# Square-sum matmuls of the norms moved later in TensorE's order, and a small projection moved ahead of a down-projection

## The chip, the cores and the metric

The kernel runs on one core of one Trainium2 chip. The metric is the device time of one execution in microseconds, lower is better. A core has TensorE (matmuls into eight PSUM banks), VectorE, ScalarE, GpSimd and the SP queue; each runs its own list of instructions in order and meets the others only at semaphores.

## The reference

Two transformer blocks of different kinds, one after the other, on 256 tokens of width 2048, all in fp32. What matters here is where the RMS norms and the residual sums stand:

```python
# first block
a = rmsnorm(h, attn_norm)                       # N_ATTN
h = h + concat(hgrn2, fox, moba of a @ w_in) @ w_out
c = rmsnorm(h, ffn_norm)                        # N_FFN
h = h + (gelu(conv(c @ w_gate)) * (c @ w_up)) @ w_down
e = rmsnorm(h, ple_norm)                        # N_PLE
h = h + sigmoid(e @ w_ple_gate) * (p @ w_ple_proj)
# second block
h2 = rmsnorm(x, attn_norm_g) * (1 + sc1) + sh1  # N_ATTN2
x = x + g1 * (concat(swa, mla of h2) @ w_out)
h2 = rmsnorm(x, mlp_norm_g) * (1 + sc2) + sh2   # N_MLP2
x = x + g2 * (relu(h2 @ w_ff1) ** 2 @ w_ff2)
return rmsnorm(x, final_norm_g)                 # N_FINAL
```

Here `rmsnorm(x, g)` is `x / sqrt(mean(x * x) + eps) * g`, the mean over the 2048 features of a token.

## The kernel before

**Layout.** The residual `x` lies in SBUF as 16 blocks of 128 features by 256 tokens. All weights form one stream of 384 *units* of 1 MB, each of two *halves* of eight 128x128 tiles. SP loads the units into four slots (`raw`) in the order in which the host packs them (`put`, at the end of the file). Each half then goes through ScalarE, which rounds it (`rnd`, line 796, `wh`), and VectorE, which makes the rest (`sub`, line 1251, `wl = raw - wh`); activations are split in the same way (a high and a low part, `xs`, `xc`, `hs`, `px`). TensorE multiplies each tile twice: `wh` by the pair (512 columns) and `wl` by the high part (256 columns), lines 489 to 493. Four slots of `wh` and `wl`; ScalarE and VectorE work three halves ahead of TensorE (`LOOK`), as far as slots come free.

**Units.** `unit(kind, ...)` is TensorE's code of one unit: "full" is one output block of 16 tiles over both halves; "eight" one block of 8 tiles per half; "quad" two blocks of 4 tiles per half (the last down-projection, K of 4 x 128). Output blocks rotate through four PSUM banks; a block waits (`s_evac`) until the one four before it has been taken. For down- and output-projections VectorE adds the block to `x` (`add_blocks`, lines 1301 and 1303); for gates ScalarE copies the low half out (`half_copy`, line 820) and VectorE adds and scales (`take_scaled`, lines 1284 and 1286).

**A norm.** The sum of squares of all 2048 features is made in four groups g of four blocks. ScalarE squares a group (`squares`, line 842), VectorE adds it down to one 128x256 tile (`square_adds`, lines 1376 and 1380) into `sqs`, which has two slots, and TensorE adds over the partitions by a matmul with ones (`square_sums`, line 502) into PS[4], for all four groups. Then ScalarE takes the root (`root`, line 858), VectorE the reciprocal (`rms_ready`, line 1292). Groups 0 to 2 are made early, while blocks of the producing projection are still coming: ScalarE at half `SQ_EIGHT` (5), 9, 13 of the last sixteen halves, VectorE one half later, TensorE one more (halves 7, 11, 15). In the last down it is SQ_QUAD = 3, in the ple gate SQ_PLE = 10 with steps of 8. N_ATTN is made from the input, beside the first two units of work.

**Normed input.** For N_ATTN, N_FFN and N_PLE the norm's factor is applied after the matmul, so that the next projection can begin with `x * gain` (`hi_x` of ScalarE, line 863; `lo_x` of VectorE, line 1360) before the root is there.

**Order around the last down.** Last up units of the ffn, last down (4 "quad" units = 8 halves), side projection `p @ w_ple_proj` (two units, four halves, TensorE lines 695 to 703; the results are copied to `mix` by ScalarE's `proj_take`, line 1139), ple gate (16 full units, `ple_in`, ScalarE's `sigmoid`, `ple_add`), then N_ATTN2. `hi_p` names in the new text the copy of `pin` to `px`, and `lo_p` its low part (line 1702). VectorE also makes products for the second block's modulation (`mods`, line 1319), one or two between halves, all through the first block.

All orders are written out by hand: each engine's list is a Python program that calls its steps at numbered halves.

Of the kernel before, what the change touches and what calls it, by code (L numbers as in the profile page):

```python
# [29 lines left out]
ALU = mybir.AluOpType  # L30
# [88 lines left out]
def build(nc, a):  # L119
    ctx = ExitStack()  # L120
    with ctx:
# [50 lines left out]
        sqs = at("sqs", [P, 2, T], T0 + 15)  # L172
# [88 lines left out]
        for name, nu, nb in (("A", U_A, 16), ("B", U_B, 19), ("C", U_C, 18), ("out", U_OUT, 16), ("outb", U_OUT, 16),  # L261
                             ("ffn1", U_FFN1, 2 * (D_FF // P) + KB * (NC1 + 1)), ("plep", U_PLEP, 8), ("pleg", U_PLEG, 16),
# [65 lines left out]
        SQ_EIGHT, SQ_QUAD, SQ_PLE = 5, 3, 10  # L328

# [130 lines left out]
        def _(pe):  # L460
# [43 lines left out]
            def early_sums(n, i, first, every):  # L504

                g, r = divmod(i - first, every)
                if r == 0 and 0 <= g < 3:
                    square_sums(n, g)
# [142 lines left out]
            def eights(name, between, n):  # L651
# [18 lines left out]
            def ups(src, n=CH, name=None, last_sum=None):  # L670
# [5 lines left out]
            ups(XFFN, name="ffn", last_sum=N_FFN)  # L676
# [85 lines left out]
            eights("mix2", mla, N_MLP2)  # L762
            square_sums(N_MLP2, 3)
# [7 lines left out]
            for u in range(KB // 2):  # L771
                unit("eight", hpairs(1), between=lambda q: early_sums(N_FINAL, 2 * u + q, SQ_EIGHT + 2, 4))
            assert c.n["h"] == 2 * UNITS and c.n["b"] == FIRST["end"][1]
# [1213 lines left out]
```

## Time and profile before

| | us |
|---|---|
| median of three runs | 2484.15 |
| lowest, highest | 2478.8, 2484.37 |
| profiled execution | 2481.15 |
| its span, first to last instruction | 2479.2 |
| TensorE busy | 2360.3 (95%) |
| VectorE busy | 1956.9 (79%) |
| ScalarE busy | 1152.7 (46%) |
| mean granted TensorE clock | 0.979 |

Busy time is the time in which an engine had an instruction in work; matmuls overlap, so a busy TensorE is not yet at its peak. In a timeline a row is one instruction or several like ones in a row: start, duration, engine, line, operation, what it writes and reads, shape, count, and in brackets how long the engine was idle before it and who ended that. A granted clock of 1.00 is 2.4 GHz, of 0.50 1.2 GHz.

### The profile page before, as it was taken

What the parts mean: (1) busy time and instruction counts of PE and PEld (TensorE: products, weight loads), DVE (VectorE), ACT (ScalarE), POOL (GpSimd) and SP (SyncE); (2) the same over time, 40 slices, a digit from 0 to 9 for tenths busy, and PEclk for the clock granted to TensorE, in tenths of its full rate; (3) what the DMA queues carried; (4) which work ended last, traced back from release to release, by engine and by line L of the source; (5) the groups of instructions that cost most, each with busy time, mean ns of one, the idle gap of its engine ahead of it and who ended that gap; (6) DMA issues with size and microseconds to landing.
All of it is one profiled execution on the core that took longest, in us unless ns stands there. A gap on an engine that the chain in (4) does not pass through costs nothing.

```text
span 2479.2 us, 37379 instructions
## 1 busy us (share of the span) xinstructions
PE 2360.3 (95%) x13254; PEld 2017.1 (81%) x13254; DVE 1956.9 (79%) x3147; ACT 1152.7 (46%) x1645; POOL 114.9 (5%) x220
## 2 busy tenths in 40 slices
PE   6989999989999999999989789898999999999997
PEld 5878787878888888888878677776888888888886
DVE  6888686889989989898987847677777777777776
ACT  5444444555545454444455435644444344434432
POOL 0100010001000000010000010000000000000000
PEclk9989999999999999999999899999999999999999
DMA  7834465468787778788756483323455555555552
GB/s 281 318 139 154 153 230 197 156 226 298 279 280 275 282 271 286 267 290 279 280 178 228 154 235 129 119 103 136 178 185 186 186 185 187 187 187 187 187 187 85
DMA packets 87112, 517.55 MB, mean 209 GB/s; under 512 B 9861, under 2 KB 10405, under 8 KB 37808
## 3 DMA queue, kind: packets, MB, share of 16 engines
q1 hardware_dynamic: 57312, 407.93, 45.6%
q0 software_dynamic: 29504, 107.37, 13.1%
q8 instruction: 91, 1.49, 0.2%
q14 instruction: 61, 0.50, 0.1%
q10 hardware_dynamic: 144, 0.26, 0.0%
HBM read 510.27 MB, written 5.25 MB: 208 GB/s over the span
## 4 chain that ended last, share of the span: by engine, by line
PE 85%; DVE 8%; ACT 3%; DMA 2%; issue 2%; SPq 0%; DVEq 0%; ACTq 0%; POOLq 0%
PE ps L492 48%; PE ps L493 24%; PE ps L490 4%; PE ps L489 2%; DVE wl L1251 2%; PE ps L550 2%; ACT wh L796 2%; DMA raw<-in_w 1%; PE ps L559 1%; PE ps L586 1%; PE ps L502 1%; DVE x L1301 1%; DVE yn L1398 1%; DVE sq L1376 0%; PE ps L568 0%
## 5 line engine op out<-in xcount | busy, mean ns | idle before, releaser
L492 PE MATMUL ps<-xs,wh 128*128 128x512 f32 x3387 | 1235.8, 405 | 26.8 <-DVE wl L1251 11.8
L796 ACT ACTIVATE wh<-raw 128x1024 fp32r<-128x1024 f32 x768 | 810.8, 1057 | 804.9 <-PE ps L490 548.1
L1251 DVE TENSOR_TENSOR wl<-raw,wh 128x1024 fp32r<-128x1024 f32 x768 | 938.2, 1223 | 264.7 <-ACT wh L796 250.0
L493 PE MATMUL ps<-xs,wl 128*128 128x256 f32 x3387 | 956.6, 282 | 0.0
L492 PEld LDWEIGHTS ps<-xs,wh 128*128 128x128 f32 x3387 | 643.8, 190 | 186.9 <-issue 22.0
L493 PEld LDWEIGHTS ps<-xs,wl 128*128 128x128 f32 x3387 | 647.3, 191 | 11.6
L492 PE MATMUL ps<-hs,wh 128*128 128x512 f32 x1504 | 544.0, 400 | 5.0 <-DVE hs L1665 3.5
L493 PE MATMUL ps<-hs,wl 128*128 128x256 f32 x1504 | 423.5, 282 | 0.0
L492 PEld LDWEIGHTS ps<-hs,wh 128*128 128x128 f32 x1504 | 284.6, 189 | 64.7 <-DVE hs L1665 3.8
L493 PEld LDWEIGHTS ps<-hs,wl 128*128 128x128 f32 x1504 | 285.8, 190 | 10.0
L1319 DVE CUSTOM_DVE_ANT_0 modraw<-modraw,cb 128x1024 f32<-128x1024 f32 x192 | 233.4, 1219 | 8.0 <-DMA modraw<-in_wmod 7.8
L1303 DVE SCALAR_TENSOR_TENSOR x<-ps,mod,x 128x256 f32<-128x256 f32 x320 | 154.9, 484 | 90.6 <-PE ps L490 84.8
L492 PE MATMUL ps<-xc,wh 128*128 128x512 f32 x616 | 221.9, 399 | 0.0
L493 PE MATMUL ps<-xc,wl 128*128 128x256 f32 x616 | 173.2, 281 | 0.0
L440 POOL DMA_DIRECT2D modraw<-in_wmod x190 | 100.3, 528 | 1250.8 <-DVE modp L1319 759.2
L492 PEld LDWEIGHTS ps<-xc,wh 128*128 128x128 f32 x616 | 115.8, 188 | 28.5
L1301 DVE TENSOR_TENSOR x<-ps,x 128x256 f32<-128x256 f32 x256 | 106.9, 423 | 30.2 <-PE ps L490 25.6
L493 PEld LDWEIGHTS ps<-xc,wl 128*128 128x128 f32 x616 | 116.3, 189 | 0.0
L820 ACT ACTIVATE tk<-ps 128x256 f32<-128x256 f32 x104 | 39.6, 381 | 130.5 <-PE ps L490 130.5
L490 PE MATMUL ps<-hs,wh 128*128 128x512 f32 x224 | 90.0, 402 | 0.0
L490 PE MATMUL ps<-xs,wh 128*128 128x512 f32 x213 | 84.7, 398 | 0.0
L1276 DVE TENSOR_REDUCE up<-ps 128x256 f32<-128x512 f32 x64 | 44.3, 692 | 38.7 <-PE ps L490 35.0
(236 smaller groups left out, 1780.5 us busy)
## 6 DMA issues: line engine op xcount, KB each, us to landing
raw<-in_w SPq DMA_DIRECT2D x383, 1024.0 KB, 5.1
modraw<-in_wmod POOLq DMA_DIRECT2D x192, 512.0 KB, 4.6
rel_rows<-rrow POOLq DMA_DIRECT2D x1, 3072.0 KB, 35.9
x<-in_x SPq DMA_DIRECT2D x4, 512.0 KB, 8.7
tbias<-rel_rows POOLq DMA_DIRECT2D x16, 128.0 KB, 6.5
out_dram<-mix SPq DMA_DIRECT2D x4, 512.0 KB, 2.7
raw<-in_w SPq DMA_DIRECT2D x2, 512.0 KB, 7.9
cb<-c_silu POOLq DMA_DIRECT2D x1, 1024.0 KB, 6.8
```

What stands on the lines that cost most here:

```text
L440: pool.dma_start(modraw[:, n:n + 1, :], a["wmod"][bass.ds(i * MOD_SLOTS + (MOD_SLOTS + n), 1), :, :] .rearrange("a p n -> p a n")).then_in ...
L489: nc.tensor.matmul(out[:, 0:T], lo[:, w], xh, start=False, stop=False)
L490: m = nc.tensor.matmul(out[:, :], hi[:, w], pair, start=False, stop=True)
L492: nc.tensor.matmul(out[:, :], hi[:, w], pair, start=s, stop=e)
L493: m = nc.tensor.matmul(out[:, 0:T], lo[:, w], xh, start=False, stop=e, skip_group_check=e)
L550: m = nc.tensor.matmul(PS[4 + J % 2][:, part(t)], l, r, start=q == 0, stop=q == len(pairs) - 1)
L796: nc.scalar.activation(wh[:, h % HS, :], raw[:, u % RAW, (h % 2) * 1024:(h % 2 + 1) * 1024], ACT.Copy).then_inc(s_round, 1)
L1251: nc.vector.tensor_tensor(wl[:, h % HS, :], raw[:, (h // 2) % RAW, (h % 2) * 1024:(h % 2 + 1) * 1024], wh[:, h % HS, :].bitcast(F32), ALU. ...
L1276: nc.vector.tensor_reduce(dst, bank()[:, :].rearrange("p (a t) -> p t a", a=2), AX.X, ALU.add).then_inc(s_evac, 1)
L1301: ins.append(nc.vector.tensor_tensor(x[:, k, :], b[:, q * T:(q + 1) * T], x[:, k, :], ALU.add))
L1303: ins.append(nc.vector.scalar_tensor_tensor(x[:, k, :], b[:, q * T:(q + 1) * T], gate[:, k:k + 1], x[:, k, :], ALU.mult, ALU.add))
L1319: nc.vector.tensor_tensor_reduce(out=modraw[:, m % 2, :], in0=modraw[:, m % 2, :], in1=cb[:, (m % 2) * 1024:(m % 2 + 1) * 1024], scale=1.0 ...
```

## The change

It does four things:

1. TensorE's ones-matmuls come later in its order. In the "eight" phases groups 0 and 1 stand at halves 9 and 13, groups 2 and 3 behind the last half (for N_FFN behind the first up unit). In the last down group 0 stands at half 7, groups 1 and 2 behind gate unit 0 and group 3 behind gate unit 1. For N_ATTN2 they stand at halves 14, 22 and 30 instead of 12, 20, 28. For N_ATTN all four stand behind the second unit.
2. `sqs` has four slots, one a group, so VectorE's wait for TensorE there refers to the norm before.
3. The side projection stands ahead of the last down in all engines' lists and in the stream of weights. The splitting of `pin` goes to the last up unit.
4. Behind the last down, the root of N_PLE stands in gate unit 2, VectorE takes gate blocks 0 and 1 in the second half of unit 2, and the sigmoids and additions of these two follow there. The product in `ple_add` alternates between two tiles.

```diff
-        sqs = at("sqs", [P, 2, T], T0 + 15)
+        sqs = at("sqs", [P, 4, T], T0 + 15)
...
+        SUM_EIGHT, SUM_QUAD, SUM_PLE = (9, 13), (7,), (14, 22, 30)
...
-                nc.tensor.matmul(PS[4][:, 0:T], ones[:, :], sqs[:, g % 2, :], start=g == 0, stop=g == 3).then_inc(s_ssq, 1)
+                nc.tensor.matmul(PS[4][:, 0:T], ones[:, :], sqs[:, g, :], start=g == 0, stop=g == 3).then_inc(s_ssq, 1)
+
+            def early_sums(n, i, at):
+
+                if i in at:
+                    square_sums(n, at.index(i))
...
-                if u < 2:
+                if u == 1:
                     pe.wait_ge(s_ones, 2)
-                    square_sums(N_ATTN, 2 * u)
-                    square_sums(N_ATTN, 2 * u + 1)
+                    for g in range(4):
+                        square_sums(N_ATTN, g)
...
-                         lambda q: early_sums(n, 2 * u + q, SQ_EIGHT + 2, 4))
+                         lambda q: early_sums(n, 2 * u + q, SUM_EIGHT))
...
-                    if j == 0 and last_sum is not None:
-                        square_sums(last_sum, 3)
+                    if j == 0 and late_sums is not None:
+                        square_sums(late_sums, 2)
+                        square_sums(late_sums, 3)
...
-            pe.wait_ge(s_h, CH * NC1 + CH_LAST)
-            c.n["hp"] += CH_LAST
-            for u in range(KB // 4):
-                unit("quad", hpairs(0, CH_LAST), between=lambda q: early_sums(N_PLE, 2 * u + q, SQ_QUAD + 2, 2))
...
-            square_sums(N_PLE, 2)
-            square_sums(N_PLE, 3)
+            pe.wait_ge(s_h, CH * NC1 + CH_LAST)
+            c.n["hp"] += CH_LAST
+            for u in range(KB // 4):
+                unit("quad", hpairs(0, CH_LAST), between=lambda q: early_sums(N_PLE, 2 * u + q, SUM_QUAD))
             for u in range(U_PLEG):
-                unit("full", XPAIR, XS["ple"] if u == 0 else None, lambda q: early_sums(N_ATTN2, 2 * u + q, SQ_PLE + 2, 8))
+                unit("full", XPAIR, XS["ple"] if u == 0 else None, lambda q: early_sums(N_ATTN2, 2 * u + q, SUM_PLE))
+                for g in ((1, 2), (3,))[u] if u < 2 else ():
+                    square_sums(N_PLE, g)
...
             eights("mix2", mla, N_MLP2)
+            square_sums(N_MLP2, 2)
             square_sums(N_MLP2, 3)
...
+            low_half()
             for n in range(2 * U_PLEP):
+                if n:
+                    proj_take(n - 1)
                 rnd(c.n["h"] + LOOK)
                 if n == 0:
-                    squares(N_PLE, 3)
-                else:
-                    proj_take(n - 1)
+                    h_hi(0, CH_LAST - 1)
                 c.n["h"] += 1
             proj_take(2 * U_PLEP - 1)
-            root(N_PLE)
...
-                step((lambda: sigmoid(j - 1)) if j else None,
+                step((lambda: sigmoid(j - 1)) if j > 2 else (lambda: root(N_PLE)) if j == 2 else None,
                      lambda q: early_squares(N_ATTN2, 2 * j + q, SQ_PLE, 8, lambda g: act.wait_ge(s_pled, 4 * g + 4)),
-                     low_half if j else None)
+                     low_half if j else None, (lambda: (sigmoid(0), sigmoid(1))) if j == 2 else None)
...
-                if 4 * n + g >= 2:
-                    dve.wait_ge(s_ssq, 4 * n + g - 1)
-                nc.vector.tensor_tensor(sqs[:, q, :], sq[:, q, 0, :], sq[:, q, 1, :], ALU.add).then_inc(s_sqs, 1)
+                if n:
+                    dve.wait_ge(s_ssq, 4 * n + g - 3)
+                nc.vector.tensor_tensor(sqs[:, g, :], sq[:, q, 0, :], sq[:, q, 1, :], ALU.add).then_inc(s_sqs, 1)
...
+            units(CH_LAST, product, first=last_down(), h_lo_of=lambda j: h_lo(0, j), nmod=1, last=lo_p)
+
+            for n in range(2 * U_PLEP):
+                half(None if n else (lambda: product(CH_LAST - 1)), after=None if n else (lambda: h_lo(0, CH_LAST - 1)))
+                c.n["b"] += 2
+            dve.wait_ge(s_evac, FIRST["down1"][1])
+
+            def summed(i):
+                lo_x("ple", (2 * i - 2, 2 * i - 1))
+                early_adds(N_PLE, i, SQ_QUAD + 1, 2)
+
+            for i in range(KB // 2):
+                half((lambda: add_blocks([2 * i - 2, 2 * i - 1])) if i else None, after=(lambda: summed(i)) if i else None)
...
+    put(tiles(i["w_ple_proj"][0]), 4)
     put(tiles(down[NC1 * n:, :]), 2)
-    put(tiles(i["w_ple_proj"][0]), 4)
```

## Rows read from the trace of the kernel before

**Rows 1.** The page, part 1: busy us (share of the span) xinstructions
```profile
PE 2360.3 (95%) x13254; PEld 2017.1 (81%) x13254; DVE 1956.9 (79%) x3147; ACT 1152.7 (46%) x1645; POOL 114.9 (5%) x220
```

**Rows 2.** Waits of TensorE: engine line <- releaser: us, times, longest us
```profile
PE ps L502 <- DVE sqs L1380: 38.7, 18, 5.6
```

**Rows 3.** Stretches: length, busy of PE, PEld, DVE, ACT, POOL, clock, DMA
```profile
480.00:536.00 56.00, 48.67 (x263) 41.70 (x264) 51.37 (x92) 26.31 (x34) 3.70 (x7) 0.97 0.60 213
1293.00:1297.00 4.00, 4.00 (x18) 3.47 (x17) 2.25 (x5) 1.85 (x3) 0.00 (x0) 0.57 0.27 113
1315.00:1406.00 91.00, 86.37 (x488) 74.42 (x486) 75.98 (x118) 46.13 (x64) 4.76 (x9) 1.00 0.63 230
```

**Rows 4.** Timeline (start us, us, what), the first two units, TensorE and VectorE
```profile
24.50 1.19 PE L502 MATMUL ps<-sqs,ones 128*128 128x256 f32 x2 [3.38 <-DVE sqs L1380]
...
33.97 0.42 DVE L1380 TENSOR_TENSOR sqs<-sq 128x256 f32<-128x256 f32 x1
...
37.10 1.02 PE L502 MATMUL ps<-sqs,ones 128*128 128x256 f32 x4
```

**Rows 5.** Timeline, second part of the first output projection, VectorE and TensorE
```profile
496.71 0.88 DVE L1301 TENSOR_TENSOR x<-ps,x 128x256 f32<-128x256 f32 x2
...
500.18 0.88 DVE L1301 TENSOR_TENSOR x<-ps,x 128x256 f32<-128x256 f32 x2
...
503.56 0.88 DVE L1301 TENSOR_TENSOR x<-ps,x 128x256 f32<-128x256 f32 x2
...
503.70 0.48 PE L502 MATMUL ps<-sqs,ones 128*128 128x256 f32 x1 [3.15 <-DVE sqs L1380]
...
536.09 0.88 DVE L1301 TENSOR_TENSOR x<-ps,x 128x256 f32<-128x256 f32 x2
...
541.45 0.59 PE L502 MATMUL ps<-sqs,ones 128*128 128x256 f32 x2
```

**Rows 6.** Timeline, between the last up unit and the last down
```profile
1260.02 0.42 DVE L1284 TENSOR_TENSOR tk<-ps,tk 128x256 f32<-128x256 f32 x1
...
1262.88 0.80 PE L492 MATMUL ps<-hs,wh 128*128 128x512 f32 x1 [3.51 <-DVE hs L1665]
```

**Rows 7.** Timeline of VectorE in the last down (1280.86: a pair of square adds begins)
```profile
1270.73 1.54 DVE L1301 TENSOR_TENSOR x<-ps,x 128x256 f32<-128x256 f32 x4
...
1280.86 0.69 DVE L1376 TENSOR_TENSOR sq<-sq 128x512 f32<-128x512 f32 x1
...
1281.93 1.21 DVE L1301 TENSOR_TENSOR x<-ps,x 128x256 f32<-128x256 f32 x3
...
1296.81 1.55 DVE L1301 TENSOR_TENSOR x<-ps,x 128x256 f32<-128x256 f32 x4 [1.75 <-PE ps L490]
1298.93 0.89 DVE L1360 SCALAR_TENSOR_TENSOR xs<-x,par,xs 128x256 fp32r<-128x256 f32 x2 [0.58 <-ACT xs L863]
```

**Rows 8.** Timeline of TensorE: side projection's first matmul, sums, gate unit 0's last tile
```profile
1296.61 0.28 PE L699 MATMUL ps<-px,wh 128*128 128x256 f32 x1
...
1308.59 1.03 PE L502 MATMUL ps<-sqs,ones 128*128 128x256 f32 x4
...
1314.88 0.40 PE L490 MATMUL ps<-xs,wh 128*128 128x512 f32 x1
```

**Rows 9.** Timeline of TensorE: last tiles of ple gate units 5 and 15
```profile
1343.14 0.39 PE L490 MATMUL ps<-xs,wh 128*128 128x512 f32 x1
...
1406.00 0.39 PE L490 MATMUL ps<-xs,wh 128*128 128x512 f32 x1
```

**Rows 10.** Timeline of TensorE: last tiles around N_MLP2's first early sum
```profile
1691.28 0.39 PE L490 MATMUL ps<-xs,wh 128*128 128x512 f32 x1
...
1695.41 0.40 PE L490 MATMUL ps<-xs,wh 128*128 128x512 f32 x1
```

**Rows 11.** Timeline of TensorE: last tiles around N_FINAL's third sum, without a stop
```profile
2459.68 0.40 PE L490 MATMUL ps<-hs,wh 128*128 128x512 f32 x1
...
2462.90 0.40 PE L490 MATMUL ps<-hs,wh 128*128 128x512 f32 x1
```

More of the change, by code:

```diff
@@ L771, in _ @@
             for u in range(KB // 2):
-                unit("eight", hpairs(1), between=lambda q: early_sums(N_FINAL, 2 * u + q, SQ_EIGHT + 2, 4))
+                unit("eight", hpairs(1), between=lambda q: early_sums(N_FINAL, 2 * u + q, SUM_EIGHT))
             assert c.n["h"] == 2 * UNITS and c.n["b"] == FIRST["end"][1]
+            square_sums(N_FINAL, 2)
             square_sums(N_FINAL, 3)
@@ L1094, in gates, with ups, hi_p @@
                              late=lambda: gelu(j - 1))
-            def ups(buf, n=CH, after=None, late=None):
+            def ups(buf, n=CH, after=None, late=None, last=None):
                 for j in range(n):
                     step(first=low_half if j or after else None, after=(lambda: h_hi(buf, j - 1)) if j else after,
-                         late=None if j else late)
+                         late=last if j == n - 1 else None if j else late)
+            def hi_p():
+                act.wait_ge(s_p, 16)
+                for k in range(2):
+                    nc.scalar.activation(XP[k][:, 0, :], pin[:, k, :], ACT.Copy).then_inc(s_yh, 1)
             def downs(after, late):
@@ L1140, in proj_take, with last_down @@
                                          PS[(FIRST["plep"][1] + 2 * n + q) % 4][:, :], ACT.Copy).then_inc(s_evac, 1)
+            low_half()
             for n in range(2 * U_PLEP):
+                if n:
+                    proj_take(n - 1)
                 rnd(c.n["h"] + LOOK)
                 if n == 0:
[L1145 to L1147 removed]
+                    h_hi(0, CH_LAST - 1)
                 c.n["h"] += 1
             proj_take(2 * U_PLEP - 1)
[L1150 removed]
+            b = FIRST["down1"][1]
+            def last_down(i):
+                if i:
+                    act.wait_ge(s_evac, b + 2 * i)
+                    hi_x("ple", (2 * i - 2, 2 * i - 1))
+                early_squares(N_PLE, i, SQ_QUAD, 2, lambda g: act.wait_ge(s_evac, b + 4 * g + 4))
+            for u in range(KB // 4):
+                step(between=lambda q: last_down(2 * u + q))
+            act.wait_ge(s_evac, b + KB)
+            hi_x("ple", (KB - 2, KB - 1))
+            squares(N_PLE, 3)
             def sigmoid(j):
@@ L1682, in gates, with units @@
                     half(after=lambda: mods(nmod, m0 if m0 is None else m0 + j * nmod))
-            def units(n, ev, first=None, lo_first=None, h_lo_of=None, nmod=0, m0=None):
+            def units(n, ev, first=None, lo_first=None, h_lo_of=None, nmod=0, m0=None, last=None):
                 for j in range(n):
@@ L1689, in units @@
                     half(after=(lambda: mods(nmod, m0 if m0 is None else m0 + j * nmod)) if nmod else None)
+                if last is not None:
+                    last()
             def downs(first, lo_first=None, gate=None, nmod=0, m0=None, each=None):
@@ L1733, in _ @@
             downs(lambda: gate_in(CH_LAST - 1), lambda: conv(CH_LAST - 1), nmod=1)
-            units(CH_LAST, product, first=last_down(), h_lo_of=lambda j: h_lo(0, j), nmod=1)
-            for j in range(KB // 4):
-                half((lambda: add_blocks([4 * j - 2, 4 * j - 1])) if j else (lambda: product(CH_LAST - 1)),
-                     after=(lambda: (lo_x("ple", (4 * j - 2, 4 * j - 1)), early_adds(N_PLE, 2 * j, SQ_QUAD + 1, 2))) if j else
-                     (lambda: (h_lo(0, CH_LAST - 1), lo_p())))
-                half(lambda: add_blocks([4 * j, 4 * j + 1]), after=lambda: lo_x("ple", (4 * j, 4 * j + 1)))
+            units(CH_LAST, product, first=last_down(), h_lo_of=lambda j: h_lo(0, j), nmod=1, last=lo_p)
[8 more added lines that the diff above has]
+                half((lambda: add_blocks([2 * i - 2, 2 * i - 1])) if i else None, after=(lambda: summed(i)) if i else None)
             tail(lambda: add_blocks([KB - 2, KB - 1]))
@@ L1743, in _ @@
             square_adds(N_PLE, 2)
-            for n in range(2 * U_PLEP):
-                half(after=(lambda: square_adds(N_PLE, 3)) if n == 0 else None)
-                c.n["b"] += 2
-            dve.wait_ge(s_evac, FIRST["pleg"][1])
-            rms_ready(N_PLE)
             def ple_in(j):
```

47 lines of the change are left out of this document (21 added, 26 removed).

## The prediction

> **What bounds the kernel now.** I read the page first. TensorE is busy for 2360.3 of 2479.2 us and VectorE for 1956.9 [rows 1]: TensorE sets the pace, with an engine close behind it. So the second view is the table of waits, for TensorE alone: its largest item by far is the ones-matmul of L502, which waited 18 times for the partial sums of VectorE, 38.7 us together [rows 2]. The third is the table of stretches, because an average over the span hides where VectorE has room. Around the first block's output projection VectorE is busy 51.37 of 56 us while TensorE has 48.67; in the ple gate it is 75.98 of 91 us [rows 3]. A removed stop is worth its length only where VectorE has such room; where it is full, I have to count VectorE's own chain instead. The fourth view is the timeline at each of the six norms. I call "half" one half unit of eight tiles. It takes TensorE 5.65/2 = 2.82 us, since 28.26 us pass over five whole units between two last tiles, 1314.88 and 1343.14 [rows 8, 9].
>
> **The change, part by part.** Arithmetic, DMA count and instruction count are the same; only orders, waits and the buffers of two small tiles differ. SP's weight queue is fed by VectorE's split of each half, and the four side-projection units only swap places in it with the four down units of the same size, so SP and POOL issue no more and no less. The `pin` load is long landed.
>
> *Start (N_ATTN).* Now TensorE ends unit 0 at 24.50 - 3.38 = 21.1 and stands before each pair of sums; all four are done at 37.10 + 1.02 = 38.1 [rows 4]. After, unit 1 runs at once (to about 26.8), then TensorE waits for the fourth partial sum, which VectorE still ends at 33.97 + 0.42 = 34.4 [rows 4], as nothing of its chain hangs on TensorE. That is up to 3 us gained. But the new stop of about 7 us will leave the clock at 1.2 GHz for the sums and the tiles behind them, which takes back some or all. Bounds 0 and 3; I take 1.0, nearer the lower end because two stops of 3 us here already lowered it.
>
> *First block's output projection (N_FFN).* TensorE's stops disappear from halves 7, 11 and 15, but VectorE is the bound. A half costs it 3.47 us with a modulation product (496.71 to 500.18) and 3.38 with a pair of square adds (500.18 to 503.56) [rows 5]. The square adds are 1.07 [rows 7], so a bare half is 2.31 and the product 1.16. From 500.18 to the last add are ten halves, five products and three pairs: 23.1 + 5.8 + 3.2 = 32.1, so 532.3 instead of 536.09 [rows 5]: 3.8 us. TensorE has half 6 done at 503.70 - 3.15 = 500.55 [rows 5]; nine halves and two sums later it is 526.8, one tile short of unit 0's end (532.1) it waits about 2.3 us for the last normed block, and then again for the fourth sum, which follows the last add by 541.45 - 536.09 = 5.4 us as now [rows 5]. The two new stops may lower the clock for some microseconds: a stretch behind a stop ran at a granted 0.57 [rows 3], where every microsecond of tiles is worth half. I take 1.0 off, bounds 0 and 2.3. Gain 2.8 (1.5 to 3.8).
>
> A rule weighed here: the Trainium skill, Perfetto Trace Analysis, section Optimization Strategies, says that when the matmul engine is idle waiting for others, one should optimize those engines. It speaks against a change that gives VectorE nothing less to do. The stretch around N_FFN agrees (VectorE 51.37 of 56 us), the ple gate does not (75.98 of 91) [rows 3]; what the rule would make of the whole stands with the first rival.
>
> *Side projection ahead of the last down (N_PLE).* Now TensorE stands 3.51 us before the down, for the last pair of `hs` [rows 6]. After, it starts the side projection when `px` is there. VectorE's two splits for it come first, at 1260.02; I take 0.42 for each from the row of the same shape, so it starts at 1260.9 [rows 6]; the product, sub and h_lo queued behind them are 0.8 us later, and their reader, the down, is 12 us away. The projection takes 1308.59 - 1296.61 = 12.0 us [rows 8], less 0.2 of a wait for ScalarE's copy: to 1272.7. The first down half ends near 1275.5; with ScalarE's last copy and a rounding ahead of VectorE's split I set VectorE's first add at 1276.0. From there VectorE is the bound: three halves and one pair of square adds are 1281.93 - 1270.73 = 11.2, so 3.38 a half and 1.07 a pair [rows 7]. Seven halves and two pairs: 25.8, so the last add starts at 1301.8. Now it starts at 1296.81 [rows 7], but there 12 us of projection still follow. The pairs of the last two blocks are ready 3.0 us later (1298.93 + 0.89 - 1296.81) [rows 7]: 1304.8. TensorE has its last down half done near 1297.7, begins gate unit 0 when a bank is free, and ends its last tile at 1304.9 instead of 1314.88 [rows 8]: 10.0 us. The deferred root and the two late sigmoids cost no time of TensorE: the fourth N_PLE sum comes after unit 1 (1312.5), ScalarE's root, VectorE's reciprocal and two takes are done near 1318, and TensorE needs the bank of block 0 only at unit 4, at 1323.8. Of what is queued behind the root, the rounding for unit 4 is the first that matters; it has 4 us. If that cover were gone, each microsecond would be one lost.
>
> *Ple gate (N_ATTN2).* From unit 0 on: 15 units of 5.65 = 84.75; three N_PLE and three N_ATTN2 sums in the stream at 0.40 each (2459.68 to 2462.90 is 3.22, less 2.82) [rows 11] are 2.4; 0.3 for a wait on the third N_PLE partial sum. 1304.9 + 87.5 = 1392.4 against 1406.00 [rows 9]. That is 13.6 us for both parts; of the 3.6 beyond unit 0, three stops go, of (62.86 - 10 x 5.65)/3 = 2.1 each (1343.14 to 1406.00 is ten units and three stops) [rows 9], and the six sums stay. Then the closing chain of N_ATTN2 is as now. Bounds 10.5 (first add and gate each 1.5 late) and 14.5.
>
> *Second block's projection (N_MLP2).* A half with a stopped sum takes 1695.41 - 1691.28 = 4.13 [rows 10], 1.31 over the bare one. Two of the three keep 0.40 in the stream, the third goes into the wait that the fourth has anyway: 2 x 0.91 + 1.31 = 3.1. VectorE's add, split and square adds fit in the two extra halves given.
>
> *Final down (N_FINAL).* Two stops of the same kind, and the third sum, which today costs 0.40 in the stream [rows 11], into the last wait: 1.8 + 0.4 = 2.2.
>
> Sum: 1.0 + 2.8 + 13.6 + 3.1 + 2.2 = 22.7. Of the profiled execution, 2481.15 us, that leaves 2458.5. The three runs' median is 3.0 above it (2484.15), so by the median it is 2461.5; I forecast 2460.0, between.
>
> **Rivals.** (1) The stops come back as waits for VectorE in the two full stretches: nothing at the start, at N_FFN and at N_PLE, and only the room elsewhere counts: 3 x 1.7 at N_ATTN2 + 3.1 + 2.2 = 10.4, so 2471. For it: VectorE's 51.37 of 56 us [rows 3]. Against: the timeline has VectorE waiting 1.75 us for TensorE before the last add [rows 7], so they now stop each other in turn. The rule of the Trainium skill above (Perfetto Trace Analysis, Optimization Strategies) would have it so. (2) Every term at its upper end, and VectorE no bound at N_FFN, so that TensorE is done there at 526.8 instead of 536.1: 3.0 + 9.3 + 14.5 + 3.1 + 2.2 = 32.1, so 2449 to 2452. For it: the clock that stays up when stops go, 0.57 behind one of them now [rows 3]. Against: VectorE's count of 32.1 us above, which has no wait in it. (3) Slower: the clock. The new stop before the side projection (1.5 us), and the waits for VectorE of 0.6 to 1.6 us before each down half, keep the clock at 1.2 GHz from 1260 to gate unit 1. Tiles there take about double: projection 21, eight halves 41, two units 21 us, 83 with the stop 84, against 52.7 in the forecast: 31 lost, 2491. It decides from the point where more than 23 of these 31 us come. Against: stops no longer than these stand in the stretch of the ple gate, at granted 1.00 [rows 3]. (4) The change does not do what it says: no sign of it; the sums do move.
>
> **How the numbers follow.** Forecast 0.73, with its own range 2452 to 2468 (bounds 15.5 and 26.6 of gain, and some 3 us that the shown runs lie to either side of the profiled one). Rival 1 0.14, rival 2 0.09, rival 3 0.03, rival 4 0.01. The range 2450 to 2470 leaves out the slow half of rival 1, most of rival 2 and rival 3, near 2 in 10. 0.3% is 7.5 us, about what a measurement of this kernel can tell from no change: faster 0.93, same 0.05, slower 0.02.
>
> **What would show it.** Right: TensorE's stops at L502 are left only at the start (7 us), at N_FFN's fourth sum (2.3) and at the closing sums of N_ATTN2, N_MLP2 and N_FINAL, which stay as they are; the side projection starts 1.5 us after the last up unit; the last add of the down comes some 29 us after the projection ends; gate units at 5.65 us without stops. Wrong: a wait of TensorE for `wl` at L492, VectorE later than 1301.8 at that add, a bank wait at gate unit 4, or granted clock under 1 anywhere between 1260 and 1390.

## The result, and the profile after

The changed kernel takes 2460.41 us (median; 2457.93 to 2462.88), the kernel before on the same chip 2481.98: a ratio of 0.991 (0.9898 to 0.9922), some 21.6 us. The profiled execution is 2457.93 us with a span of 2456.2, against 2481.15 and 2479.2: 23.2 us. In the changed file TensorE's sums are L504 (502 before), VectorE's adds L1306 (1301), its splits of normed blocks L1365 (1360), its square adds L1381 and L1385 (1376 and 1380), its products for the modulation L1324 (1319), gate tiles L491 and L492 (489 and 490).

The page, part 1 (as [rows 1]), and two items of TensorE's waits, us, times, longest (as [rows 2]):

```profile
PE 2351.1 (96%) x13254; PEld 2010.6 (82%) x13254; DVE 1952.9 (80%) x3147; ACT 1151.5 (47%) x1645; POOL 114.9 (5%) x220
PE ps L504 <- DVE sqs L1385: 19.2, 6, 5.6
PE ps L597 <- DVE sec L1291: 5.4, 1, 5.4
```

A stop here is a wait of TensorE. 18 stops at the ones-matmul have become 6, and 38.7 us have become 19.2; a new one of 2.29 us at N_FFN stands at L491 and is not among them. VectorE has the same number of instructions and the same busy time to 4 us. So the change removed waits, not work, and it did not make VectorE faster.

Stretches (as [rows 3]), then the ple gate and the time behind N_FFN's last sum:

```profile
480.00:536.00 56.00, 52.38 (x294) 45.12 (x294) 51.69 (x94) 28.85 (x39) 4.22 (x8) 0.99 0.66 227
1303.00:1390.00 87.00, 87.00 (x494) 75.56 (x493) 79.07 (x123) 49.31 (x69) 4.75 (x9) 1.00 0.66 240
535.20:542.00 6.80, 4.78 (x14) 4.01 (x15) 5.87 (x10) 4.25 (x6) 0.41 (x1) 0.50 0.50 171
```

In the gate TensorE is busy for 87.00 of 87 us (86.37 of 91 before, [rows 3]). Around the output projection VectorE is as full as before, 51.69 of 56 us, and TensorE does 31 matmuls more in the same stretch. The third row is the cost: the clock is at 0.50, 1.2 GHz, for 6.8 us around and behind the new stops.

Timeline at the start, TensorE (as [rows 4]), and the stop that ends the first input projection:

```profile
28.66 0.70 PE L504 MATMUL ps<-sqs,ones 128*128 128x256 f32 x2 [1.67 <-DVE sqs L1385]
33.28 2.28 PE L504 MATMUL ps<-sqs,ones 128*128 128x256 f32 x4 [3.92 <-DVE sqs L1385]
...
120.67 1.94 PE L597 MATMUL ps<-ident,sec 128*128 128x128 f32 x8 [5.44 <-DVE sec L1291]
```

At N_FFN (as [rows 5]), the last add and square adds of VectorE and the stops of TensorE:

```profile
532.10 0.88 DVE L1306 TENSOR_TENSOR x<-ps,x 128x256 f32<-128x256 f32 x2
534.09 0.39 PE L491 MATMUL ps<-xc,wl 128*128 128x256 f32 x1 [2.29 <-DVE xc L1365]
536.01 0.69 DVE L1381 TENSOR_TENSOR sq<-sq 128x512 f32<-128x512 f32 x1 [1.98 <-ACT sq L844]
537.22 1.22 PE L504 MATMUL ps<-sqs,ones 128*128 128x256 f32 x2 [2.07 <-DVE sqs L1385]
```

From the last up unit to the closing of N_ATTN2 (as [rows 6 to 9]): first matmul of the side projection, first and last add of the down, last tile of gate unit 0, the three sums behind it, last tile of unit 15, closing stop:

```profile
1258.81 0.39 PE L695 MATMUL ps<-px,wh 128*128 128x256 f32 x1 [1.46 <-DVE px L1709]
...
1273.91 1.53 DVE L1306 TENSOR_TENSOR x<-ps,x 128x256 f32<-128x256 f32 x4
...
1299.68 1.53 DVE L1306 TENSOR_TENSOR x<-ps,x 128x256 f32<-128x256 f32 x4
...
1303.11 0.40 PE L492 MATMUL ps<-xs,wh 128*128 128x512 f32 x1
1303.34 0.94 PE L504 MATMUL ps<-sqs,ones 128*128 128x256 f32 x3
...
1390.23 0.40 PE L492 MATMUL ps<-xs,wh 128*128 128x512 f32 x1
1396.18 1.22 PE L504 MATMUL ps<-sqs,ones 128*128 128x256 f32 x2 [5.55 <-DVE sqs L1385]
```

No stop is left between unit 0's first tile and 1396. The closing stop of N_ATTN2 is still there. The stretch from the last up unit to the first gate tiles:

```profile
1257.00:1303.00 46.00, 41.32 (x260) 36.12 (x259) 37.40 (x73) 27.60 (x42) 0.53 (x1) 1.00 0.47 169
```

The closing sum of N_FINAL, before and then changed:

```profile
2466.67 0.70 PE L502 MATMUL ps<-sqs,ones 128*128 128x256 f32 x2 [3.37 <-DVE sqs L1380]
```

```profile
2443.19 1.22 PE L504 MATMUL ps<-sqs,ones 128*128 128x256 f32 x2 [2.94 <-DVE sqs L1385]
```

**Where the time went, stage by stage.** One pair of traces turned out to be too few. I cut each trace at the same last tiles: at 415.3 us in the changed kernel's time (the end of the first block's attention inputs), 478.7 (first part of the output projection), 545.3 (second gate unit behind N_FFN), 1257.0 (last up unit), 1315.7 (ple gate unit 2), 1412.9 (first unit of block 2), 1531.6, 1719.9 (first unit behind N_MLP2) and 2439.4 (the last tile of all). The first column is the time at which the first cut is reached, the others are lengths, the last is all from the first cut to the end of the span.

| kernel (profiled execution) | first cut | to 479 | N_FFN, to 545 | ffn, to 1257 | N_PLE, to 1316 | gate, to 1413 | to 1532 | N_MLP2, to 1720 | to 2439 | rest |
|---|---|---|---|---|---|---|---|---|---|---|
| before | 415.79 | 63.07 | 68.44 | 711.68 | 67.21 | 102.48 | 120.20 | 192.14 | 721.90 | 2063.40 |
| e12: before again | 418.00 | 63.55 | 68.56 | 711.68 | 67.12 | 102.67 | 119.61 | 192.34 | 721.94 | 2063.74 |
| changed | 415.27 | 63.41 | 66.60 | 711.68 | 58.77 | 97.16 | 118.70 | 188.34 | 719.48 | 2040.96 |
| e10: changed again | 415.28 | 63.19 | 66.74 | 711.79 | 58.69 | 97.17 | 118.36 | 188.58 | 719.88 | 2041.21 |
| e7: start as before | 419.65 | 63.33 | 66.60 | 711.69 | 58.68 | 97.16 | 118.74 | 188.47 | 719.89 | 2041.37 |
| e11: e7 again | 417.04 | 63.11 | 66.66 | 711.78 | 58.79 | 97.06 | 118.54 | 188.63 | 719.82 | 2041.22 |
| e1: sums only | 415.58 | 62.01 | 65.83 | 711.78 | 63.95 | 97.16 | 118.73 | 188.08 | 719.62 | 2043.45 |
| e2: order only | 417.64 | 63.31 | 68.50 | 711.68 | 63.20 | 103.26 | 119.84 | 192.08 | 722.21 | 2060.56 |
| e3: fewer products at the start | 412.11 | 63.18 | 66.65 | 711.68 | 58.69 | 98.15 | 120.69 | 188.09 | 720.08 | 2043.86 |
| e4: none ahead of N_FFN | 415.53 | 63.32 | 59.62 | 711.79 | 58.67 | 101.58 | 119.33 | 188.75 | 719.93 | 2039.27 |
| e5: fourth sum later | 419.85 | 63.38 | 63.24 | 713.08 | 58.67 | 97.16 | 120.55 | 188.52 | 720.14 | 2041.56 |
| e6: more in the down | 415.01 | 62.04 | 65.82 | 711.78 | 67.04 | 97.06 | 117.89 | 188.98 | 720.45 | 2047.69 |
| e8: e4, products in the ffn | 417.42 | 63.32 | 59.50 | 721.70 | 58.69 | 97.15 | 119.06 | 188.42 | 720.14 | 2044.79 |
| e9: e8 and e3 | 411.58 | 63.15 | 59.50 | 717.15 | 63.73 | 97.17 | 121.93 | 188.52 | 719.89 | 2047.87 |

Two executions of one kernel agree to 0.35 us in the rest, but differ by up to 2.6 us at the first cut. The rest is 2063.57 before and 2041.09 after (means of two): 22.5 us are the change's own behind the first cut.

### The profile page after: what moved, and what is told of

It is laid out like the page before. It is cut to its first block, busy times and chain, and to the rows that moved or that the text cites. A ratio compares the mean times of both kernels' runs of the same rounds, so it can differ in the third digit from the quotient of the medians.

```text
span 2456.2 us, 37374 instructions
## 1 busy us (share of the span) xinstructions
PE 2351.1 (96%) x13254; PEld 2010.6 (82%) x13254; DVE 1952.9 (80%) x3147; ACT 1151.5 (47%) x1645; POOL 114.9 (5%) x220
## 4 chain that ended last, share of the span: by engine, by line
PE 83%; DVE 9%; DMA 3%; ACT 3%; issue 2%; SPq 0%; POOLq 0%; DVEq 0%; ACTq 0%
PE ps L494 47%; PE ps L495 23%; PE ps L492 4%; DVE wl L1256 2%; PE ps L491 2%; PE ps L551 2%; DMA raw<-in_w 1%; DMA modraw<-in_wmod 1%; ACT wh L798 1%; PE ps L560 1%; DVE x L1306 1%; PE ps L587 1%; DVE modraw L1324 1%; DVE yn L1403 1%; PE ps L504 0%
## 5 line engine op out<-in xcount | busy, mean ns | idle before, releaser
L1324 DVE CUSTOM_DVE_ANT_0 modraw<-modraw,cb 128x1024 f32<-128x1024 f32 x192 | 233.3, 1218 | 13.9 <-DMA modraw<-in_wmod 13.8
L1306 DVE TENSOR_TENSOR x<-ps,x 128x256 f32<-128x256 f32 x256 | 106.7, 422 | 21.1 <-PE ps L492 16.9
L492 PE MATMUL ps<-hs,wh 128*128 128x512 f32 x224 | 89.2, 398 | 0.0
L492 PE MATMUL ps<-xs,wh 128*128 128x512 f32 x213 | 84.9, 399 | 0.0
```

Of the source, the lines that this page charges most:

```text
L492: m = nc.tensor.matmul(out[:, :], hi[:, w], pair, start=False, stop=True)
L1306: ins.append(nc.vector.tensor_tensor(x[:, k, :], b[:, q * T:(q + 1) * T], x[:, k, :], ALU.add))
L1324: nc.vector.tensor_tensor_reduce(out=modraw[:, m % 2, :], in0=modraw[:, m % 2, :], in1=cb[:, (m % 2) * 1024:(m % 2 + 1) * 1024], scale=1.0 ...
```

## Experiments

My theory of the gain was the prediction's own sum: stops go where VectorE has room, and where it has none its own chain sets the time. The runs ask which half of the change earns it, whether VectorE really is the bound in the two full stretches, and what the start is worth.

**e1, the sums without the order.** The kernel before, with all later sums and four slots; side projection behind the down as it was. At N_PLE the later sums stand behind the side projection.

```diff
             for u in range(KB // 4):
-                unit("quad", hpairs(0, CH_LAST), between=lambda q: early_sums(N_PLE, 2 * u + q, SQ_QUAD + 2, 2))
+                unit("quad", hpairs(0, CH_LAST), between=lambda q: early_sums(N_PLE, 2 * u + q, SUM_QUAD))
...
-            square_sums(N_PLE, 2)
-            square_sums(N_PLE, 3)
+            for g in (1, 2, 3):
+                square_sums(N_PLE, g)
```

> The kernel before with the four sqs slots and all later places of the ones-matmuls, but the old order of last down and side projection. Theory (VectorE's chain bounds the down, the stops only stretched it): its adds of the last down take 25.8 us from the first to the last instead of 29.5, TensorE leaves the down about 7 us earlier, gate unit 0 ends about 6.6 us earlier (near 1306 to 1308 on before's scale); with 1.8 at N_FFN, nothing kept of the start, 5.2 at N_ATTN2, 3.5 at N_MLP2 and 2.2 at the end that is 19 us: 2463 against 2482. Rival (the terms as the prediction lists them, the down's gain belonging to the new order): 12 to 13 us, 2469.

Measured 2465.21 us (2460.7 to 2469.55), ratio 0.9934 (0.992 to 0.9948).

**e2, the order without the sums.** The changed kernel, with every sum at its old place.

```diff
-        SUM_EIGHT, SUM_QUAD, SUM_PLE = (9, 13), (7,), (14, 22, 30)
+        SUM_EIGHT, SUM_QUAD, SUM_PLE = (7, 11, 15), (5, 7), (12, 20, 28)
...
-                for g in ((1, 2), (3,))[u] if u < 2 else ():
+                for g in ((2,), (3,))[u] if u < 2 else ():
```

> The changed kernel with the new order of side projection and last down, but the ones-matmuls at their old places wherever there is one (halves 7, 11, 15; 12, 20, 28; 5 and 7 in the down; after units 0 and 1 of phase A). Theory: a stop before down half 7 hands TensorE to the gate about 2.2 us later than in the changed kernel, so gate unit 0 ends some 7 us earlier than before, and nothing else is gained: 7 us, 2475. Rival (the order carries the down's whole gain, 10 us, and the low clock of two stretches more): 10 to 12 us, 2471.

Measured 2480.82 us (2478.16 to 2485.6), ratio 0.9991 (0.9982 to 1.0). TensorE in its last down and behind gate unit 0, and a stretch there:

```profile
1292.78 1.22 PE L504 MATMUL ps<-sqs,ones 128*128 128x256 f32 x2 [3.54 <-DVE sqs L1382]
...
1303.51 0.70 PE L504 MATMUL ps<-sqs,ones 128*128 128x256 f32 x2 [1.80 <-DVE sqs L1382]
...
1291.70:1298.50 6.80, 5.72 (x18) 4.87 (x19) 4.34 (x9) 1.86 (x3) 0.00 (x0) 0.50 0.44 157
```

The starts of VectorE's first and last adds of the last down, e1 and then e2:

```profile
1263.76 1.55 DVE L1304 TENSOR_TENSOR x<-ps,x 128x256 f32<-128x256 f32 x4 [4.04 <-PE ps L491]
...
1289.55 1.54 DVE L1304 TENSOR_TENSOR x<-ps,x 128x256 f32<-128x256 f32 x4
```

```profile
1278.07 1.54 DVE L1303 TENSOR_TENSOR x<-ps,x 128x256 f32<-128x256 f32 x4
...
1307.04 1.55 DVE L1303 TENSOR_TENSOR x<-ps,x 128x256 f32<-128x256 f32 x4 [0.20 <-PE ps L492]
```

For e1 the theory's total held: 17.7 us by the medians (the kernel before took 2482.87 on that chip), and 20.1 in the rest (2063.57 - 2043.45), against 19. Not all of its terms did. The adds take 25.8 us as expected, but gate unit 0 ends only 3.2 us earlier behind the last up unit (55.9 to 52.7), where 6.6 were expected, and the two stages up to 545 gave 4.0 instead of 1.8. That these make up for each other is luck. In these two stages e1 is some 2 us ahead of the changed kernel, and so is e6, which has the changed kernel's own code there; so these stages scatter too. For e2 both expectations were too high: 2.1 us by the medians, 3.0 in the rest. The side projection ahead of the down does win 4.0 us up to gate unit 2 (67.2 to 63.2), but a sum at its old place then stops TensorE for 3.54 us and takes the clock to 0.50 for 6.8 us, and the gate loses 0.7.

What each half does at N_PLE shows in VectorE's adds. From the first to the last they take 29.5 us before, 29.0 in e2, 25.8 in e1 and 25.8 in the changed kernel: the later sums shorten this chain, the order does not. From the last add to the end of gate unit 0 it is 18.1 us before and 18.4 in e1, where the projection still stands between, but 5.2 in e2 and 3.4 in the changed kernel; the first add comes 8.6 us later for it. In the two stages together, sums alone win 8.6 us (169.7 to 161.1), the order alone 3.3, both 13.8, which is 1.9 more than the two by themselves.

**e6, is VectorE the bound in the last down?** The changed kernel with one modulation product more in seven of its halves, and seven fewer in the gate.

```diff
             def summed(i):
                 lo_x("ple", (2 * i - 2, 2 * i - 1))
                 early_adds(N_PLE, i, SQ_QUAD + 1, 2)
+                mods(1)
```

> The changed kernel with one modulation product more in each of seven halves of the last down, seven fewer in the ple gate: the same work in another place. Theory (VectorE bounds the down): the adds from first to last take 7 x 1.15 = 8.1 us longer, gate unit 0 ends 8 us later, nothing comes back in the gate: 8 us slower than the changed kernel. Rival (TensorE bounds it, or the bank waits do and VectorE has room): under 2 us.

Measured 2467.03 us (2463.54 to 2470.05), ratio 0.994 (0.9921 to 0.9958). The stage is 67.04 instead of 58.73 us: 8.3 for seven products, 1.19 each, as the theory has it (8.1). TensorE's waits from 1257 to 1303 us, in e6 and then in the changed kernel:

```profile
PE ps L494 <- DVE x L1306: 6.3, 4, 2.5
```

```profile
PE ps L494 <- DVE x L1306: 1.7, 2, 1.4
```

**e4, is it the bound ahead of N_FFN?** No products in the first output projection; they go to the ple gate.

```diff
-            eights("mix", J_SWA, moba, N_FFN, nmod=1, into_next="ffn")
+            eights("mix", J_SWA, moba, N_FFN, nmod=0, into_next="ffn")
```

> The changed kernel, with VectorE's eight modulation products taken out of the sixteen halves ahead of N_FFN; they go to the ple gate, which gets eight more. Theory (VectorE sets the end of the first block's output projection): at least the three to five products since VectorE fell behind are worth 1.16 us each, so the first gate unit behind N_FFN ends 3.5 to 4.5 us earlier, at about 530; TensorE then is the bound there. In the ple gate VectorE has 15 us of room in 91 and eight products take 9.3, so at most 1 us is lost: 2457 (2456 to 2458) against the changed kernel's 2460.4. Rival (something else holds N_FFN, such as the transfers or ScalarE): 0 at N_FFN and the time stays at 2460 to 2461.

Measured 2457.78 us (2456.47 to 2461.28), ratio 0.99 (0.9885 to 0.9915). TensorE at N_FFN's last sums and at the closing of N_ATTN2, and an item of VectorE's waits in the gate (us, times, longest):

```profile
532.19 1.02 PE L504 MATMUL ps<-sqs,ones 128*128 128x256 f32 x4
...
1393.78 1.22 PE L504 MATMUL ps<-sqs,ones 128*128 128x256 f32 x2 [9.98 <-DVE sqs L1385]
...
DVE modraw L1324 <- DMA modraw<-in_wmod: 2.6, 4, 1.3
```

The stage of N_FFN shrinks by 7.0 us, to 59.6, more than expected: both stops (4.4) and the low clock go, and TensorE now is the bound (58.20 of 59.60 us busy). That is VectorE as the cause there, shown: the loads of the eight products go away with them, but VectorE waited for no load between 480 and 545 us in the changed kernel. But 4.4 us come back in the gate, where I had expected at most 1. I had counted room from VectorE's busy time before (15 us of 91); in the changed kernel the gate is shorter, 87 us with 79.07 busy, and a product also has to wait for its weights.

**e5, the fourth N_FFN sum one unit later.**

```diff
-                    if j == 0 and late_sums is not None:
-                        square_sums(late_sums, 2)
-                        square_sums(late_sums, 3)
+                    if j < 2 and late_sums is not None:
+                        square_sums(late_sums, 2 + j)
```

> The changed kernel, with only the fourth N_FFN sum one unit later, behind the second gate unit. Theory (the stop of 2.07 us at the fourth sum is a wait that the next unit can cover, and the lowered clock behind the two stops goes with it): 2.0 to 3.5 us less at the end of the third gate unit, so 2457 to 2458.5 against 2460.4. Rival (the whole of VectorE's chain stands behind the sum: root, reciprocal and the take of unit 0 come later, and the bank of unit 0 is missing four units on): 0 to 3 us more, 2460 to 2463, with a wait of TensorE for a bank at the fifth gate unit.

Measured 2460.97 us (2457.57 to 2463.08), ratio 0.9904 (0.9889 to 0.9919). The third and the fourth sum:

```profile
539.11 0.60 PE L504 MATMUL ps<-sqs,ones 128*128 128x256 f32 x2
...
546.71 0.59 PE L504 MATMUL ps<-sqs,ones 128*128 128x256 f32 x2
```

The stop goes and the stage is 3.4 us shorter, at the theory's upper end; but the ffn behind it is 1.4 longer and the input projection of block 2 another 2.0 (120.55 against 118.53), and in the rest nothing remains (2041.56). Theory right at its place, rival right in total, though not by the bank wait it named: TensorE's only wait from 545 to 600 us is 0.6 us for `wl`. What takes the 3.4 us again is not shown.

**e8 and e9, the products elsewhere.** e8 is e4 with the eight in every second of the first sixteen ffn units; e9 is e8 with one product a unit in the first stage too, four of those six in the last ffn units.

```diff
-            gates(CH, nmod=1, rooted=N_FFN)
+            gates(CH, nmod=lambda j: 1 + j % 2, rooted=N_FFN)
```

> As the kernel without modulation products ahead of N_FFN, but the eight go to every second of the first sixteen units of the first ffn, where VectorE is idle for 0.56 us in each unit of 5.65, and the ple gate keeps as many as in the changed kernel. Theory (the 4.4 us won at N_FFN came back in the gate because the eight products filled VectorE there): the closing stop of N_ATTN2 is 5.6 us again instead of 9.98, and the gain at its end is 4.4 us; the second block's input projection, which starts that much earlier, takes 1 to 2 of them. So 2455.0 (2454.5 to 2457.5) against 2457.8 with them in the gate and 2460.4 for the changed kernel. Rival (VectorE's share of 0.90 in the ffn leaves no room either): four or more microseconds lost between 547 and 640, and 2460 again.

> As the kernel with the eight products in the first ffn, and one product a unit in the first stage as well (six fewer there; four go to the last units of the first ffn, two to the gate). Theory (the stop near 120 us is VectorE's arrival, which two products every second unit delay): 3 to 4 us more won at 160 us, of which the second block's input projection takes 1 to 2 again: 2453.5 (2452 to 2455.5). Rival (what comes earlier into the second block is lost there, because a chain of transfers ends last): as the kernel without this, within 0.5 us.

Measured 2461.14 us (2459.25 to 2463.88), ratio 0.9901 (0.9882 to 0.992), and 2459.48 us (2458.3 to 2461.11), ratio 0.9896 (0.9877 to 0.9915). e8's closing stop is 5.55 again, as the theory had it, but the ffn is 10.0 us longer: the rival. Waits of VectorE from 547 to 700 us, the longest of them, and the same item in the changed kernel, where it waits for `wh` instead:

```profile
DVE modraw L1324 <- DMA modraw<-in_wmod: 8.3, 7, 3.8
DVE wl L1256 <- ACT wh L798: 0.2, 1, 0.2
...
584.70 1.22 DVE L1324 CUSTOM_DVE_ANT_0 modraw<-modraw,cb 128x1024 f32<-128x1024 f32 x1 [3.77 <-DMA modraw<-in_wmod]
```

```profile
DVE wl L1256 <- ACT wh L798: 8.7, 22, 0.6
```

This closes the sum for e8: eight products of 1.22 are 9.8, their waits for weights 8.3, and 8.5 of the idle time is used up: 9.6, measured 10.0. In e9 those waits are 3.8 and the idle time falls by 8.1: 5.5, measured 5.5, all of it in the first sixteen units; the four products in the last ffn units cost nothing up to the last up unit. So the idle 0.56 us a unit was real room and was used, and what the stage grew by is nearly the waits for the transfers of the products, in a stretch where the DMA engines are 0.8 busy.

e9 also tests what I feared of the clock. TensorE at the side projection, and a stretch:

```profile
1255.59 0.58 PE L695 MATMUL ps<-px,wh 128*128 128x256 f32 x1 [3.81 <-DVE px L1709]
...
1254.90:1261.80 6.90, 6.21 (x29) 6.21 (x30) 3.29 (x7) 1.10 (x3) 0.53 (x1) 0.51 0.88 289
```

With the stop at 3.81 us instead of 1.46 the clock is at 0.51 for 6.9 us, and the stage is 5.0 us longer: 2.35 of stop and some 3 of clock. In total e9 is neither what its theory had (2453.5) nor within 0.5 us of e8: the first cut comes 3.7 us earlier than in the changed kernel, and the rest is 6.8 longer, with 7.2 won at N_FFN and 5.4, 5.0 and 3.4 lost in the ffn, at N_PLE and in the input projection of block 2.

**e3, the stop near 120 us.** The changed kernel, one product a unit in the first stage, six more in the gate.

```diff
-            fulls(U_A, keep(S1), lambda j: 2 - j % 2 if j >= MOD_UNIT else 0, entry, late=True)
+            fulls(U_A, keep(S1), lambda j: 1 if j >= MOD_UNIT else 0, entry, late=True)
```

> The changed kernel with one modulation product a unit in phase A instead of one and two in turn; the six left over fall to the ple gate, which makes all that remain. Theory (the 2 us won at the start are lost again because VectorE waits for the modulation loads in phase A): VectorE's waits for these loads before 120 us (about 10 us in sum) go, TensorE's stop at 120.7 us falls from 5.4 to under 3.4 us and 1.5 to 3 us of the span go; the gate has 15 us of room for 7 us of products. Rival (that stop is the chain of the recurrent mixer itself): the stop stays at 5.4 or grows by what TensorE gets ahead, the span stays within 0.5 us, or grows by 1 to 3 us in the gate.

Measured 2457.79 us (2456.3 to 2461.34), ratio 0.9902 (0.9885 to 0.992). The stop:

```profile
116.87 1.06 PE L597 MATMUL ps<-ident,sec 128*128 128x128 f32 x8 [1.67 <-DVE sec L1291]
```

It falls from 5.44 to 1.67 us, and to 1.7 in e9 too, where no kernel with the old products has less than 3.35; so it is VectorE's arrival. VectorE no longer waits for modulation weights up to 160 us in either. 3 us are kept at the first cut, and 2.8 lost again in the rest: 1.0 in the gate, whose closing stop is longer by that, and 2 in the input projection of block 2.

**e7, e10, e11, e12, the start.** e7 is the changed kernel with the N_ATTN sums in pairs behind units 0 and 1, as before; e10, e11 and e12 repeat the changed kernel, e7 and the kernel before.

```diff
-                if u == 1:
+                if u < 2:
                     pe.wait_ge(s_ones, 2)
-                    for g in range(4):
-                        square_sums(N_ATTN, g)
+                    square_sums(N_ATTN, 2 * u)
+                    square_sums(N_ATTN, 2 * u + 1)
```

> The changed kernel, with the four N_ATTN sums in their old places, two behind unit 0 and two behind unit 1. Theory (the two microseconds that the change wins at the start are given back at the end of the first stage, where VectorE arrives at the same time in any case): unit 2 ends 2.0 us later, at 43.4, the stop near 120 us is shorter by as much (3.4 instead of 5.4), and the total stays within 0.5 us of 2460.4. Rival (my forecast: a gain at the start stays in the total): 1 to 2 us more, 2461.5 to 2462.5.

> The changed kernel once more, nothing edited, for the spread of the starts between two profiled executions of one kernel. Theory (the arrival of the modulation weights decides when the first stage ends): the last tile of unit 2 lies within 0.5 us of 41.35, but those near 152.6 and 255.4 lie up to 3 us elsewhere, and from 480 us on to the end the distance stays as it is at 415; total 2460.4. Rival (the start is as repeatable as the rest): all within 0.5 us, so that the 2.0 us won at the start and lost near 120 us are the change's own.

> The changed kernel with the N_ATTN sums in their old places, once more, nothing edited against the run before of that name. Theory (each program has a first stage of its own that repeats, as the changed kernel's two executions do to 0.2 us): unit 2 at 43.7, then 154.4, 258.2 and 419.7 again, 4 us behind the changed kernel at 419, and 2462 to 2463. Rival (the first stages scatter from one execution to the next): unit 2 at 43.7, the other three anywhere within 4 us of the first execution, and the total nearer 2460.4.

> The kernel before once more, nothing edited. Theory (as above): last tiles at 43.4, 150.4, 254.3 and 415.8 as in its first profile, within 0.3 us. Rival: the last three up to 4 us elsewhere. The difference of the sums at the start is only as sure as this agreement. Total 2482 either way.

Medians: e7 2462.68 us (2461.85 to 2464.75), e10 2458.57 (2458.16 to 2460.01), e11 2462.18 (2457.58 to 2465.56), e12 2483.9 (2479.28 to 2485.53; ratio 0.9994, 0.9985 to 1.0003). From the first pair of traces I had read that the 2.0 us won at unit 2 (43.39 to 41.35) are lost near 120 us, since the stop there is 5.44 us and was 3.35. e10 agreed to 0.1 us at the first cut and seemed to confirm it. e11 and e12 took it away: the same two kernels reach the first cut 2.6 us earlier and 2.2 us later than they had, with stops near 120 of 3.84 instead of 5.59 and 4.41 instead of 3.35. Of the executions whose start is the changed one (changed, e10, e1, e4, e5, e6, e8) the mean at the first cut is 416.3, of those with the old start (before, e12, e2, e7, e11) 417.6. So at this cut the start is worth about 1.3 us, with 415.0 to 419.9 and 415.8 to 419.7 as the spread; by these alone zero is not excluded. Two other readings say that it is not zero. Unit 2 ends at 41.2 to 42.1 us in the seven executions with the changed start and at 42.3 to 43.7 in the five with the old one: 1.5 us by the means, without overlap. And the median of all eight timed executions of the changed kernel (with e10) is 2459.4, of all ten with only the start as before (e7 and e11) 2462.4, though on different chips. What makes the first stage scatter is probably the arrival of the modulation weights (VectorE waits 6.9 to 13.6 us for them up to 160 us). Without these waits, in e3 and e9, the first cut lies at 412.11 and 411.58; but the waits do not order the other twelve, so this is not shown.

The best variants, e3 and e4 at 2457.8, lie 0.8 and 2.6 us below the changed kernel's own two medians (2458.57 and 2460.41), with intervals of their ratios that overlap: too little to call either faster.

## Why the prediction was right, point by point

| part | forecast | measured |
|---|---|---|
| start | 1.0 (0 to 3) | 1.3, spread larger than that |
| N_FFN | 2.8 (1.5 to 3.8) | 1.8 (68.50 to 66.67) |
| N_PLE and N_ATTN2 | 13.6 (10.5 to 14.5) | 13.8 (169.74 to 155.90) |
| input projection of block 2 | 0 | 1.4 (119.9 to 118.5) |
| N_MLP2 | 3.1 | 3.8 (192.24 to 188.46) |
| N_FINAL | 2.2 | 2.2 (721.92 to 719.68) to the last tile, 1.7 to the end |

Measured are the means of the kernel before and e12, and of the changed kernel and e10. Behind the start the forecast adds up to 21.7 and the measurement to 22.5, of which 1.4 lie in a stage that the forecast left out.

- **N_PLE.** VectorE's chain was the right thing to count. The changed kernel comes to this stage 2.0 us earlier than before (1256.97), which I had not deducted in the absolute times. With it my first add is 1274.0 (measured 1273.91), the last 1299.8 (1299.68), unit 0's last tile 1302.9 (1303.11) and unit 15's 1390.4 (1390.23). e6 shows that this chain is the bound, at 8.3 us for seven products. The root and the two sigmoids behind unit 2 cost TensorE nothing, as costed. The clock stayed at 1.00 all the way, as the forecast needed. e1 and e2 add what the sum could not say: the sums alone earn 8.6 of the 13.8, the order alone 3.3.
- **N_FFN.** The last add was forecast at 532.3 and stands at 532.10, the stops at 2.3 and 2.3 and stand at 2.29 and 2.07. The step that was mis-sized is the clock: I took 1.0 (0 to 2.3). The row of the stretch 535.2 to 542 has TensorE busy for 4.78 us at 0.50, which is 2.4 us lost, just over my upper bound. e4 gives what the place is worth without VectorE, 68.5 to 59.6 or 8.9 us, close to the 9.3 of the second rival. The 1.8 itself is as sure as that stage repeats: e1 and e6, with the same code there, need 65.8 and not 66.7.
- **N_MLP2.** The stopped sums gave 3.2. The closing of the norm and the unit behind it gave another 0.5 (1720.56 to 1741.01 is 20.45, 1700.01 to 1719.94 is 19.93), which I had taken as unchanged. The closing pair of ones-matmuls takes 1.22 us before and 0.70 after, in both executions of each; with the wait ahead of it that is the whole 0.5.
- **N_FINAL.** Here it is the other way round. To the last tile the gain is the forecast one, but the closing pair takes 0.70 us before and 1.22 after (again in both executions of each), and from the last tile to the end of the span it is 16.8 us instead of 16.3. So this 0.5 and that of N_MLP2, neither of them in the sum, cancel by luck.
- **Input projection of block 2.** Not in the sum. It varies from 117.9 to 121.9 us among the kernels, most where VectorE's products or the arrival were moved (e3, e5, e9), so its 1.4 us may not be the change's. What sets it stays open: ScalarE waits 11.4 to 13.4 us there for `raw` in each trace I read.
- **Start.** The size was right within what can be told. The one stop of 7 us became two, of 1.67 and 3.92 us; the four sums are done at 35.56 us and not at 38.1, and the clock did fall, to 0.50 from 32 to 36 us. How much of the gain lasts to the end of the first stage is less sure: a single pair of traces can't show 1 us there.
- **Rivals.** The first (waits for VectorE replace the stops) fell at N_PLE and mostly at N_FFN: two waits of 4.4 us in all came in place of its stops, of 6.7. The rule of the Trainium skill (Perfetto Trace Analysis, Optimization Strategies: optimize the engines that the matmul engine waits for) is half right here: at N_FFN relieving VectorE gives 7 us more at that place (e4), at N_PLE reordering alone took TensorE's waits between the last up unit and the gate from 9.0 us to 4.6 with VectorE's work unchanged, and e6 shows VectorE as the bound of what is left. The second rival needed 32 us, and its N_FFN gain of 9.3 came only in e4, with VectorE relieved. The third (clock) did not happen, since the stop was 1.46 us and the clock stayed at 1.00; e9, with a stop of 3.81 us at the same place, and e2, with one of 3.54 us in the down, show that it is real, at some 3 us of low clock and not 31.
- **Slips.** The prediction has four side-projection units swapping with four down units; they are two units (four halves) and four. Nothing in the sum used it. And its lower bound of gain, 15.5, does not follow from its terms: 0 + 1.5 + 10.5 + 3.1 + 2.2 is 17.3. The measured time lies well inside either.

The medians differ by 21.6 us, the profiled executions by 23.2; my 22.7 lies between. Of that last 1 us nothing can be said, with first stages that scatter by 2.6.

## What to carry to other kernels

A matmul that reduces another engine's result is a synchronisation point: put it where that result is surely there, give each partial result its own slot, and count the supplier's own chain of instructions to learn where the gain ends. An engine's idle share is room only in the schedule as it then stands, and work that needs a transfer can cost the wait for it on top, as it did in e8: price a moved instruction as its time plus the wait for its data less the idle time it meets. Before reading a gain of 2 us in one stage from two traces, take the trace of each kernel twice and compare stage lengths, not times since the start.

## What the runs showed of the hardware

- Stops of TensorE and the granted clock behind them. 1.46 us ahead of the side projection left it at 1.00; 3.81 us there (e9) and 3.54 us in the down (e2) took it to 0.51 and 0.50 for 6.9 and 6.8 us. At N_FFN two stops of 2.29 and 2.07 us close together did the same. In e6 one of 2.54 us, which followed two of 1.5, was followed by a clock of 0.62 over 4 us, and in the kernel before one of 1.82 us, which came 9.7 us after one of 3.47, by 0.53 over 3 us. So in these traces the length of one stop does not tell by itself. The time of a stop can count twice: the stage behind the 3.81 us stop grew by 5.0 us for 2.35 us more of stop.
- The loads of modulation weights, asked for at one and a half times the old rate in the ffn (e8), made VectorE wait 8.3 us over seven of them, in a stretch where it had not waited for them at all.
- In two executions of the same kernel (three pairs) the stages behind the first cut repeat to 0.0 to 0.6 us, and the first 415 us to 0.0, 2.2 and 2.6.
